# Hybrid decoder step on one core: third expert's weight loads moved behind the first gathers, softmax's maximum and difference moved behind the one-hots

## Chip, cores and metric

The kernel runs on one core of a Trainium2 chip. The metric is the device time of one execution in microseconds. TensorE has two clock levels, 1.2 and 2.4 GHz; the profile gives the granted clock as a share of the higher one.

## What is computed

One layer of a decoder for 536 tokens (16 meta, 512 prompt, 8 sample tokens) of width 1024: a mixer of two branches, then a hierarchical mixture of experts. The change touches only the step from one to the other.

```python
x = x + m                                   # m: mixer output
u = rmsnorm(x, norm2_g)
lg = u @ router_group_w + router_group_b    # 4 groups
le = u @ router_expert_w + router_expert_b  # 4 groups x 4 experts
grp = argmax(lg); p_grp = softmax(lg)[grp]
top_v, top_i = top_k(le[grp], 2); w_top = softmax(top_v)
h = silu(u @ expert_w_gate) * (u @ expert_w_up)      # 16 experts, 1024 x 256
x = x + sum over the token's 2 experts of  p_grp * w_top * (h @ expert_w_down)
y = rmsnorm(x, final_norm_g)
```

## The kernel before

**Two parts.** A first block (the mixer, about 705 us) is written as a list of steps that each engine follows in its own order. Its last steps are the routing. Then comes a loop over rounds (one round here) with the expert passes.

**Routing.** The 536 tokens lie on 128 partitions in 5 tiles. `ranked` (L779) compares the logits of groups and experts with each other and finds each token's experts; for the second part of the tiles (`i` = 1) it ends with softmax's maximum and difference (L811 to L813), on which ACT's exponential waits (semaphore `d_ll`). `placed` (L815) reads each token's place within its expert from PE's sums. `slotted` (L824) makes the one-hot rows (L839) and the pass codes (L835). `slot_products` (L873) on PE multiplies the two, ten small products, and `slots_known` (L842) makes of them the list `ids`: which token stands in which of the 12 passes' 128 slots. Each expert has 96 slots, so a pass of 128 slots holds parts of two experts. All this DVE work stands one behind the other, each operation waiting for the one before.

**Gathers.** The normalised rows u2 were stored to `u_dram` rows (`u_rows` in the profile), x2 to `x_rows`. Once `ids` is known, POOL gathers the rows of passes 0 and 1 (`first_rows`, L886, one indirect DMA of 128 rows x 4 KB each, L883). All later gathers wait in the loop for the buffer of the gather two before (L2065 to L2072).

**Passes on PE.** `to_channels` (L2113) transposes the gathered rows, `gate_up` (L2125) multiplies them by the expert's gate and up weights, `hidden_in` and `down` (L2139, L2147) do the rest. For all but the last three passes ACT scales the result, and POOL adds it to `x_rows` by an indirect DMA (L2076, "the scatter"). When all nine scatters have landed, SP reads `x_rows` back (L2044), POOL gathers the rows that the last three passes still change (L2083), DVE adds and norms them, and the result goes to `out_y` (L2049, L2106).

**Weights.** `load_expert` (L772) asks for two transfers, gate/up (2 MB, L767) and down (1 MB, L770). Six buffers hold six experts. All are asked for on SP's queue, which works through this order:

```python
for i in range(2):
    load_expert(sp, i)            # L982
...
for t in range(2): x2_out(t)      # L997
for t in range(TT): u2_out(t)     # L999
job_done(sp, ("j_out", KD - 1, 1))
load_expert(sp, 2)                # L1002
for t in range(2, TT): x2_out(t)  # L1003
```

In the loop SP waits for both first gathers (L2025), then asks for experts 3, 4 and 5, and from expert 6 on for each as a pass frees its buffer (L2032 to L2038). Where more than one round is needed, a block at the loop's end (L2372) asks for the first three experts of the next.

Of the kernel before, what the change touches and what calls it, by code (L numbers as in the profile page):

```python
# [17 lines left out]
ALU = mybir.AluOpType  # L18
ACT = mybir.ActivationFunctionType
AX = mybir.AxisListType  # L20
# [3 lines left out]
KD = D // P  # L24
# [347 lines left out]
def hybrid_step(nc, I, O):  # L372

    with ExitStack() as ctx:
# [197 lines left out]
        def job_done(eng, step):  # L572
            eng.wait_ge(s_job, JOBS[step] + 1)
# [33 lines left out]
        def bc(a, n):  # L607
            return a.unsqueeze(len(a.shape)).broadcast_to(list(a.shape) + [n])
# [163 lines left out]
        def load_expert(eng, i):  # L772
            load_gu(eng, i)
            load_dn(eng, i)
# [4 lines left out]
        def ranked(dve, v, run, tt, i):  # L779

            t0, t1 = ((0, EARLY), (EARLY, TT))[i]
            rows = slice(t0 * (1 + NG), t1 * (1 + NG))
            if i:
                dve.wait_ge(d_rt, 2)
                run(v.reciprocal(rstd[:, EARLY:TT], rstd[:, EARLY:TT]), d_rc)
            dve.wait_ge(d_lg, i + 1)
            for t in range(t0, t1):
                n = rows_of(t)
                run(v.scalar_tensor_tensor(lg[0:n, t, :], logits(t, n), rstd[0:n, t:t + 1], bias[0:n], ALU.mult, ALU.add))
            x = ll[:, rows]  # L790
            me = bc(x, 4)
            other = x.unsqueeze(2).broadcast_to(list(x.shape[:2]) + [4, 4])
            tt(gt[:, rows], other, me, ALU.is_gt)
            tt(eq[:, rows], other, me, ALU.is_equal)
            tt(eq[:, rows], eq[:, rows], cc("tie", 4, 4).unsqueeze(1).broadcast_to([P, x.shape[1], 4, 4]))
            tt(gt[:, rows], gt[:, rows], eq[:, rows], ALU.add)
            run(v.tensor_reduce(rank.rearrange("p t r e -> p (t r) e")[:, rows], gt[:, rows], AX.X, ALU.add))
            run(v.tensor_scalar(ga[:, t0:t1], rank[:, t0:t1, 0, :], 0.5, None, ALU.is_lt))
            tt(ga[:, t0:t1], ga[:, t0:t1], bc(cc("valid")[:, t0:t1], 4))
            for a in range(2):  # L800
                fv = ff[:, t0:t1, a, :].rearrange("p t (g e) -> p t g e", g=NG)
                run(v.scalar_tensor_tensor(fv, rank[:, t0:t1, 1:1 + NG, :], float(a), bc(ga[:, t0:t1], 4), ALU.is_equal,
                                           ALU.mult))
            tt(selb[:, t0:t1, :], ff[:, t0:t1, 0], ff[:, t0:t1, 1], ALU.add, s=d_sel)

            j = slice(2 * t0, 2 * t1)
            tt(tq[:, t0:t1], ff[:, t0:t1], cc("code").unsqueeze(1).unsqueeze(1).broadcast_to([P, t1 - t0, 2, NE]))
            run(v.tensor_reduce(first[:, j], tq[:, t0:t1].rearrange("p t a e -> p (t a) e"), AX.X, ALU.add))
            run(v.tensor_tensor(first[:, j].rearrange("p (t a) -> p t a", a=2), first[:, j].rearrange("p (t a) -> p t a", a=2),
                                bc(lost[:, t0:t1], 2), ALU.add))  # L810
            if i:  # L811
                run(v.tensor_reduce(mx, ll, AX.X, ALU.max))
                tt(ll, ll, bc(mx, 4), ALU.subtract, s=d_ll)  # L813

        def placed(dve, v, run, tt, i):  # L815

            t0, t1 = ((0, EARLY), (EARLY, TT))[i]
# [83 lines left out]
        def _(sp):  # L901
# [96 lines left out]
                x2_out(t)  # L998
            for t in range(TT):  # L999
                u2_out(t)  # L1000
            job_done(sp, ("j_out", KD - 1, 1))
            load_expert(sp, 2)  # L1002
            for t in range(2, TT):  # L1003
                x2_out(t)

# [614 lines left out]
        def _(dve):  # L1620
# [30 lines left out]
            for step in STEPS:  # L1651
# [258 lines left out]
                elif kind == "j_bc":  # L1910
                    n = step[1]
                    p0, p1, c0, c1 = UNITS[n]
                    job_done(dve, step)
                    for p in range(p0, p1):
                        y = ly[:, p, c0:c1]
                        run(v.scalar_tensor_tensor(y, y, vv("lnw", p), un_ps(kind, n)[:, p - p0, :], ALU.mult, ALU.mult),
                            free if p == p1 - 1 else None)
                elif kind in ("ln_w", "ln_b"):
                    _, n, p = step
                    _, p1, c0, c1 = UNITS[n]  # L1920
                    if n < 6:
                        job_read(dve, ("j_bc", n))
                    for q in [p] if n < 6 else range(p, p1):
                        x, y = tmp[:, q, c0:c1], ly[:, q, c0:c1]
                        if kind == "ln_w":
                            stt(y, y, vv("lnw", q), x, ALU.mult, ALU.mult)
                        else:
                            stt(y, y, vv("lnb", q), bon[:, q, c0:c1], ALU.add, ALU.add)
                elif kind == "ln_g":
                    n = step[1]  # L1930
                    tt(un(ly, n), un(ly, n), un(g_f, n), s=s_ya)
                elif kind == "j_ba":
                    _, m, hf = step
                    job_done(dve, step)
                    if hf == 0:
                        for q in range(2):
                            job_read(dve, ("j_proj", GA0 + m, q))
                            job_read(dve, ("j_bb", m, q))
                    stt(sga[:, m, cols(hf)], sga[:, m, cols(hf)], 1.0, job_ps(step), ALU.add, ALU.mult, s=free)
                    job_read(dve, step)  # L1940
                    tt(merged[:, m, cols(hf)], merged[:, m, cols(hf)], sga[:, m, cols(hf)], ALU.add, s=s_mg)
                elif kind == "j_out":
                    _, m, hf = step
                    dve.wait_ge(s_xr, 16)
                    job_done(dve, step)
                    stt(u[:, m, cols(hf)], job_ps(step), 0.5, u[:, m, cols(hf)], ALU.mult, ALU.add, s=free)
                elif kind == "rt_in":
                    run(v.memset(eps2[:, :], EPS))
                    run(v.tensor_scalar(lost[:, :], cc("valid"), -4096.0, 4096.0, ALU.mult, ALU.add))
                    run(v.memset(ssq, 1.0))  # L1950
                    run(v.memset(lg, 0.0))
                    run(v.memset(cnt, 0.0))
                    run(v.tensor_copy(trib[:, :], cc("tri")))
                    run(v.tensor_copy(oneb[:, :], ones))
                    dve.wait_ge(d_ld, 48)
                    o2 = VEC["norm2_g"]
                    run(v.memset(wr[:, :, 20:32], 0.0))
                    run(v.memset(logt[:, T:TT * P], 0.0))
                    run(v.memset(wsel, 0.0))
                    run(v.memset(wsel[:, 20:21], 1.0))  # L1960
                    tt(quad, ident[:, 0:21], ident[:, 32:53], ALU.add)
                    for i in range(2, 4):
                        tt(quad, quad, ident[:, 32 * i:32 * i + 21], ALU.add)
                    tt(wr[:, :, 0:20], wr[:, :, 0:20], bc(vec[:, o2:o2 + KD], 20), s=d_wr)
                elif kind == "x2":
                    dve.wait_ge(d_rt, 1)
                    run(v.reciprocal(rstd[:, 0:2], rstd[:, 0:2]), d_rc)
                elif kind == "ranked":
                    ranked(dve, v, run, tt, 0)
                elif kind == "slotted":  # L1970
                    placed(dve, v, run, tt, 0)
                    slotted(v, run, 0)
                elif kind == "route":
                    ranked(dve, v, run, tt, 1)
                    placed(dve, v, run, tt, 1)
                    slotted(v, run, 1)
                    slots_known(dve, v, run, at_first)
                    run(v.tensor_reduce(cnt[:, 0:1], bank(6)[:, PS0 + NE * TT:PS0 + NE * TT + NE], AX.X, ALU.max))
                    tt(cnt[:, 1:ROUNDS], cnt[:, 0:1].broadcast_to([P, ROUNDS - 1]), cc("more"), ALU.is_gt)
                    run(v.tensor_reduce(cnt[:, 6:7], cnt[:, 1:ROUNDS], AX.X, ALU.add))  # L1980
                    run(v.tensor_scalar(n_rounds[:, :], cnt[:, 6:7], 1.0, None, ALU.add), d_n)
# [33 lines left out]
        with nc.Fori(0, rounds) as r:  # L2015
# [4 lines left out]
            with nc.Block(no_gpsimd_drain=True) as block:  # L2020
                @block.sync
                def _(sp):
                    sp.wait_ge(d_x, 3)
                    sp.wait_ge(d_lt, 3)
                    for q in range(2):  # L2025
                        at_least(sp, q_g[q], EVERY, 16)
                    load_expert(sp, 3)
                    sp.dma_start(O["retp"], ret_st).then_inc(z_out[1], 16)
                    load_expert(sp, 4)
# [335 lines left out]
            with nc.If(r + 1 < rounds):  # L2365
# [3 lines left out]
                with nc.Block(no_gpsimd_drain=True) as block:  # L2369
                    @block.sync  # L2370
                    def _(sp):
                        for i in range(3):  # L2372
                            load_expert(sp, i)

                    @block.gpsimd
# [85 lines left out]
```

## Time and profile before

| | |
|---|---|
| median of 3 runs | 875.0 us (874.85 to 876.51) |
| the profiled execution: its own time | 876.24 us |
| its span, first to last instruction | 874.7 us |
| mean granted TensorE clock | 0.977 |
| PE busy | 839.2 us (96%) |
| DVE / ACT / POOL busy | 367.6 / 183.7 / 37.6 us |
| DMA moved | 125.29 MB |

Times in the trace count from the span's start. Gather and weight transfers are asynchronous: the row of an issuing instruction shows how long the engine took to ask, and "to landing" is the time from there until the last of the 16 DMA engines has reported. In the chain of waits a DMA row runs from issue to landing. "SPq" is SyncE's queue, "PEld" a weight load into the array. "arena" is the one large on-chip buffer in which most tiles lie.

### The profile page before, as it was taken

How to read it: one execution, taken by the hardware profiler on the slowest of the kernel's cores; microseconds unless marked ns; L12 is line 12 of the kernel's file. 1: busy time of each engine (PE TensorE's matmuls, PEld its weight loads, DVE VectorE, ACT ScalarE, POOL GpSimd, SP SyncE). 2: the span in 40 equal slices, each digit the busy share in tenths (PEclk: the TensorE clock that was granted, in tenths of full speed). 3: DMA queues.
4: the chain of work that ended last, by engine and by line, in shares of the span. 5: the costliest groups of instructions: out<-in, count | busy, mean ns of one | idle time of the engine just before them, and what ended most of it. 6: DMA issues, size and time to landing. Idle time of an engine off the chain costs nothing.

```text
span 874.7 us, 20496 instructions
## 1 busy us (share of the span) xinstructions
PE 839.2 (96%) x9014; PEld 591.5 (68%) x9014; DVE 367.6 (42%) x729; ACT 183.7 (21%) x418; POOL 37.6 (4%) x34
## 2 busy tenths in 40 slices
PE   8999999999999999999999999998999859999994
PEld 6877777787788777777777777776887723333331
DVE  6343333347779554454543343217413441111135
ACT  2111112142322211111111331220004311111134
POOL 0000000000000000000000000000000011122223
PEclk9999999999999999999999999989999959999997
DMA  9432321422211110111013101046362289999965
GB/s 353 153 99 73 107 91 49 170 72 97 73 56 54 37 46 31 39 39 31 35 39 100 50 27 51 3 154 249 146 268 97 73 330 423 384 394 394 391 227 224
DMA packets 30343, 125.29 MB, mean 143 GB/s; under 512 B 5824, under 2 KB 8416, under 8 KB 25392
## 3 DMA queue, kind: packets, MB, share of 16 engines
q1 hardware_dynamic: 25936, 113.03, 34.1%
q0 software_dynamic: 4320, 10.95, 4.3%
q8 instruction: 72, 1.18, 0.5%
q14 instruction: 15, 0.12, 0.0%
HBM read 106.31 MB, written 20.25 MB: 145 GB/s over the span
## 4 chain that ended last, share of the span: by engine, by line
PE 90%; DVE 4%; DMA 3%; issue 2%; ACT 1%; POOL 0%; POOLq 0%; DVEq 0%; ACTq 0%
PE psum L1036 43%; PE psum L1347 9%; PE psum L2135 8%; PE psum L2167 4%; PE psum L1169 2%; PE psum L1208 1%; PE psum L1303 1%; PE psum L1221 1%; PE psum L1125 1%; PE psum L1113 1%; PE psum L2118 1%; PE psum L1218 1%; PE psum L1057 1%; DMA arena<-x_rows,ids 1%; PE psum L1189 1%
## 5 line engine op out<-in xcount | busy, mean ns | idle before, releaser
L1036 PE MATMUL psum<-arena 128*128 128x268 f32 x1600 | 398.8, 397 | 0.2
L1036 PEld LDWEIGHTS psum<-arena 128*128 128x128 f32 x1600 | 294.1, 190 | 75.1 <-issue 12.1
L1638 DVE TENSOR_TENSOR arena<-psum,arena 128x256 f32<-128x256 f32 (+6 forms) x178 | 74.9, 426 | 202.3 <-PE psum L1221 52.3
L1441 ACT ACTIVATE arena<-psum 128x268 f32<-128x268 f32 (+6 forms) x184 | 71.6, 397 | 373.6 <-PE psum L1036 272.9
L1638 DVE TENSOR_TENSOR arena<-arena 128x256 f32<-128x256 f32 (+11 forms) x204 | 102.1, 500 | 42.9 <-ACT arena L1441 31.0
L1347 PE MATMUL psum<-arena 128*128 128x268 f32 x384 | 90.5, 390 | 0.9 <-DVE arena L1641 0.9
L2135 PE MATMUL psum<-arena 128*32 128x512 f32 (+1 forms) x640 | 87.5, 610 | 2.9 <-DVE arena L2288 2.9
L1347 PEld LDWEIGHTS psum<-arena 128*128 128x128 f32 x384 | 71.2, 189 | 16.3 <-DVE arena L1641 1.7
L2288 DVE TENSOR_TENSOR arena<-psum,arena 128x256 f32<-128x256 f32 (+1 forms) x36 | 24.1, 691 | 111.8 <-ACT arena L2202 97.3
L2135 PEld LDWEIGHTS psum<-arena 128*32 128x32 f32 (+1 forms) x640 | 25.5, 117 | 61.3 <-issue 59.7
L1641 DVE SCALAR_TENSOR_TENSOR arena<-arena 128x8 f32<-128x8 f32 (+6 forms) x93 | 49.0, 527 | 12.2 <-DMA arena<-arena 9.1
L883 POOL DMA_INDIRECT arena<-u_rows,ids x12 | 12.5, 1038 | 770.6 <-DVEq L1984 704.2
L1441 ACT ACTIVATE arena<-arena 128x268 f32<-128x268 f32 (+10 forms) x65 | 25.4, 412 | 93.1 <-PE psum L1359 59.1
L2167 PE MATMUL psum<-arena 128*32 128x512 f32 (+1 forms) x288 | 40.2, 596 | 0.0
L1543 ACT ACTIVATE arena<-psum 64x256 f32<-64x256 f32 (+1 forms) x54 | 20.4, 378 | 85.1 <-PE psum L1189 55.0
L1641 DVE SCALAR_TENSOR_TENSOR arena<-arena,psum 128x268 f32<-128x268 f32 (+1 forms) x36 | 18.8, 522 | 27.3 <-PE psum L1036 12.7
L1641 DVE SCALAR_TENSOR_TENSOR arena<-psum,arena 128x268 f32<-128x268 f32 (+2 forms) x23 | 10.4, 451 | 44.6 <-PE psum L1347 39.4
L2167 PEld LDWEIGHTS psum<-arena 128*32 128x32 f32 (+1 forms) x288 | 10.8, 115 | 21.3 <-issue 21.3
L2202 ACT ACTIVATE arena<-psum 128x256 f32<-128x256 f32 x12 | 4.6, 385 | 79.1 <-PE psum L2135 79.1
L2118 PE MATMUL psum<-arena 128*128 128x128 f32 x96 | 13.5, 286 | 7.3 <-DMA arena<-u_rows,ids 7.3
L1208 PEld LDWEIGHTS psum<-arena 32*32 32x32 f32 (+1 forms) x1072 | 11.7, 105 | 12.3 <-issue 12.3
L2217 ACT ACTIVATE arena<-psum,arena 128x1024 f32<-128x1024 f32 x9 | 10.0, 1116 | 37.5 <-PE psum L2167 37.5
(196 smaller groups left out, 677.8 us busy)
## 6 DMA issues: line engine op xcount, KB each, us to landing
arena<-in_w_gu SPq DMA_DIRECT2D x16, 2048.0 KB, 20.8
arena<-in_w_in SPq DMA_DIRECT2D x46, 512.0 KB, 3.5
arena<-in_w_dn SPq DMA_DIRECT2D x16, 1024.0 KB, 19.5
arena<-in_w_out SPq DMA_DIRECT2D x2, 2048.0 KB, 12.3
arena<-in_x SPq DMA_DIRECT2D x8, 268.0 KB, 4.8
arena<-arena SPq DMA_DIRECT2D x16, 134.0 KB, 3.3
arena<-in_x SPq DMA_DIRECT2D x1, 2144.0 KB, 11.1
arena<-in_rets SPq DMA_DIRECT2D x1, 2048.0 KB
```

The lines of the kernel that those rows point to most:

```text
L1036: last = mm(ps, wt[:, i % NW, k, :], rhs[:, k, cols(hf)], start=(k == 0), stop=(k == nk - 1))
L1169: mm(o, bk[full, q, i, p, 0:w], ar[full, q, p, :, 0:w], start=True, stop=True)
L1208: last = mm(psum[g, 2304 + H * p:2304 + H * p + n], ab[c % 2][g, p, 0, rd], tp[c % 2][g, 0, p, 0:n], start=True, stop=True)
L1347: last = mm(ps, w[:, k, :], x[:, k, cols(hf)], start=(k == 0), stop=(k == nk - 1))
L1441: run(nc.scalar.activation(out, in_, fn, **kw), s)
L1543: nc.scalar.activation(tok[c % 2][part, i, :, :], src, ACT.Copy).then_inc(s_toks if s else s_act, 1)
L1638: run(v.tensor_tensor(out, a, b, op), s)
L1641: run(v.scalar_tensor_tensor(out, a, sc_, b, op0, op1), s)
L2118: last = nc.tensor.transpose(psum[:, P * k:P * (k + 1)], ug[:, e % 2, P * k:P * (k + 1)], ident)
L2135: last = mm(bank(2 + i % 2)[part], ue[:, i % 2, k, part], w_gu[x % NWE][:, k, :], start=(k == 0), stop=(k == KD - 1))
L2167: last = mm(bank(down_bank(e) + q)[part], hht(e)[:, f, part], w_dn[x % NWE][:, f, 512 * q:512 * q + 512], start=(f == 0), stop=(f == 1))
L2288: v.tensor_tensor(out, x, y, op).then_inc(s, 1)
```

## The change

`load_expert(sp, 2)` and the wait for the mixer's last product ahead of it leave the first block; the load goes to the loop's SP block, behind the wait for both gathers and ahead of expert 3. The block for a further round loads two experts instead of three. `ranked` loses its last two operations, and the step "route" makes them between `slotted` and `slots_known`.

```diff
@@ -808,10 +808,6 @@
             run(v.tensor_tensor(first[:, j].rearrange("p (t a) -> p t a", a=2), first[:, j].rearrange("p (t a) -> p t a", a=2),
                                 bc(lost[:, t0:t1], 2), ALU.add))
-            if i:
-                run(v.tensor_reduce(mx, ll, AX.X, ALU.max))
-                tt(ll, ll, bc(mx, 4), ALU.subtract, s=d_ll)
-
         def placed(dve, v, run, tt, i):
@@ -998,8 +994,6 @@
             for t in range(TT):
                 u2_out(t)
-            job_done(sp, ("j_out", KD - 1, 1))
-            load_expert(sp, 2)
             for t in range(2, TT):
                 x2_out(t)
@@ -1974,6 +1968,8 @@
                     ranked(dve, v, run, tt, 1)
                     placed(dve, v, run, tt, 1)
                     slotted(v, run, 1)
+                    run(v.tensor_reduce(mx, ll, AX.X, ALU.max))
+                    tt(ll, ll, bc(mx, 4), ALU.subtract, s=d_ll)
                     slots_known(dve, v, run, at_first)
@@ -2024,6 +2020,7 @@
                     for q in range(2):
                         at_least(sp, q_g[q], EVERY, 16)
+                    load_expert(sp, 2)
                     load_expert(sp, 3)
                     sp.dma_start(O["retp"], ret_st).then_inc(z_out[1], 16)
                     load_expert(sp, 4)
@@ -2369,7 +2366,7 @@
                     @block.sync
                     def _(sp):
-                        for i in range(3):
+                        for i in range(2):
                             load_expert(sp, i)
```

SP's queue before, from the end of the mixer into the loop (in_w_gu and in_w_dn are one expert's gate/up and down weights):

```order
82 L995 DMA u_rows<-arena 128x1024 x4
83 L995 DMA u_rows<-arena 24x1024
84 L767 DMA arena<-in_w_gu 128x4096
85 L770 DMA arena<-in_w_dn 128x2048
86 L991 DMA x_rows<-arena 128x1024 x2
87 L991 DMA x_rows<-arena 24x1024
```

The same stretch of SP's queue with the change, on to the first requests in the loop (L2010 to L2014 are the round count, the loop's entry and the wait for the gathers):

```order
83 L991 DMA u_rows<-arena 24x1024
84 L987 DMA x_rows<-arena 128x1024 x2
85 L987 DMA x_rows<-arena 24x1024
86 L1980 UNCONDITIONAL_BRANCH
87 L2010 TENSOR_LOAD n_rounds
88 L2010 ISA x2
89 L2011 UNCONDITIONAL_BRANCH
90 L2017 UNCONDITIONAL_BRANCH
91 L2014 ISA
92 L767 DMA arena<-in_w_gu 128x4096
93 L770 DMA arena<-in_w_dn 128x2048
94 L767 DMA arena<-in_w_gu 128x4096
```

The pair of transfers has gone from between the stores; behind the wait for the gathers expert 2's pair (92, 93) now stands ahead of expert 3's (from 94).

DVE at the end of the routing with the change (L835 makes the one-hots, L841 to L843 are `slots_known`):

```order
541 L835 TENSOR_TENSOR onehot<-arena 128x768
542 L1971 TENSOR_REDUCE arena<-arena 128x25
543 L1632 TENSOR_TENSOR arena<-arena 128x100
544 L841 COPY arena<-psum 128x24
545 L842 SCALAR_TENSOR_TENSOR arena<-arena 128x12
546 L843 TENSOR_SCALAR ids<-arena 128x12
```

The maximum (L1971) and the difference (L1632) stand between the one-hots and the copy that waits for PE's products; before, nothing stood there.

## Rows read from the trace of the kernel before

**Rows 1.** Page, busy us, share of the span, instructions.
```profile
PE 839.2 (96%) x9014; PEld 591.5 (68%) x9014; DVE 367.6 (42%) x729; ACT 183.7 (21%) x418; POOL 37.6 (4%) x34
```

**Rows 2.** Chain of waits, routing to pass 0: start us, us, what.
```profile
698.46 0.27 DVE arena L812
698.75 0.27 DVE arena L1638
...
701.45 0.97 DVE onehot L839
...
702.55 0.43 PE psum L878 x10
...
704.64 8.21 DMA arena<-u_rows,ids
712.90 1.98 PE psum L2118 x8
...
716.38 9.58 PE psum L2135 x64
```

**Rows 3.** Timeline of SP's queue around the gathers: start us, us, instruction.
```profile
697.05 0.54 SPq L767 DMA_DIRECT2D arena<-in_w_gu  x1
...
698.13 1.70 SPq L991 DMA_DIRECT2D x_rows<-arena  x3
...
713.74 0.35 SPq L767 DMA_DIRECT2D arena<-in_w_gu  x1
```

**Rows 4.** Stretches: us, busy of PE, PEld, DVE, ACT, POOL, PEclk, DMA share, GB/s.
```profile
697.00:698.00 1.00, 0.30 (x11) 0.30 (x12) 0.86 (x5) 1.00 (x2) 0.00 (x0) 0.74 1.04 401
712.00:713.00 1.00, 0.10 (x1) 0.10 (x2) 0.00 (x0) 0.00 (x0) 0.00 (x0) 0.50 0.41 160
730.00:735.00 5.00, 5.00 (x26) 1.63 (x24) 0.00 (x0) 0.00 (x0) 0.00 (x0) 1.00 1.04 440
```

**Rows 5.** Single transfers by line: down 11, gate/up 14, gate/up 15, down 15.
```profile
L770 SPq DMA_DIRECT2D arena<-in_w_dn x1: 328/328/328, 787.6 to 787.6; - x1
DMA to landing us min/median/max: 22.8/22.8/22.8
...
L767 SPq DMA_DIRECT2D arena<-in_w_gu x1: 362/362/362, 799.9 to 799.9; - x1
DMA to landing us min/median/max: 26.8/26.8/26.8
...
L767 SPq DMA_DIRECT2D arena<-in_w_gu x1: 328/328/328, 806.5 to 806.5; - x1
DMA to landing us min/median/max: 31.1/31.1/31.1
...
L770 SPq DMA_DIRECT2D arena<-in_w_dn x1: 328/328/328, 823.0 to 823.0; - x1
DMA to landing us min/median/max: 19.5/19.5/19.5
```

**Rows 6.** Timeline and chain, gate/up products of passes 9 and 11, then the end.
```profile
822.94 7.09 PE L2135 MATMUL psum<-arena 128*32 128x512 f32 x64
...
843.21 7.09 PE L2135 MATMUL psum<-arena 128*32 128x512 f32 x64
...
836.95 6.79 DMA x_rows<-arena,ids
843.96 2.51 SPq L2044 DMA_DIRECT2D arena<-x_rows  x5
...
847.41 8.99 DMA arena<-x_rows,ids
```

**Rows 7.** Stretch of one us near the end, columns as in rows 4.
```profile
836.00:837.00 1.00, 1.00 (x6) 0.29 (x5) 1.00 (x1) 0.11 (x1) 0.05 (x1) 1.00 0.25 107
```

**Rows 8.** Page, DMA issues, indirect transfers of 512 KB: count, median us to landing.
```profile
x_rows<-arena,ids POOLq DMA_INDIRECT x12, 11.1
out_y<-arena,ids POOLq DMA_INDIRECT x3, 3.4
```

## The prediction

> **What bounds the kernel now.** I read the page first, then the chain of waits through the routing, the SP queue, DMA by stretches, single transfers with their landings, and last the chain of the end. PE is busy 839.2 us of 874.7 [rows 1], so time comes only from a hole in it, and only if what lies behind the hole can be earlier too. The chain [rows 2] shows the hole: the two DVE operations that the change moves (L812 at 698.46, L1638 at 698.75), the one-hots, PE's products, then 8.21 us in which nothing but the first gather's landing is waited for, then 1.98 us of transposes at 712.90, and at 716.38 the products of pass 0. What the gather waits behind is in [rows 3]: SP asks at 697.05 for the third expert (3 MB: gate/up 2048 KB, down 1024 KB) and at 698.13 for three pieces of x_rows; the fourth expert follows at 713.74, once both first gathers have landed. In [rows 4] the DMA engines are full at 697 (share 1.04) and run empty at 712 (0.41): the gathers land with the last of this backlog.
>
> The other end matters as much. In the pass loop the DMA share is 1.04 at 730 to 735 with 440 GB/s [rows 4]: the weight stream keeps up, but with growing lag. Landings [rows 5]: gate/up 14 asked for at 799.9 took 26.8 us, gate/up 15 at 806.5 took 31.1 (landed 837.6), the last down weights at 823.0 took 19.5 (landed 842.5). By [rows 7] the share at 836 is only 0.25 while those are still under way: about 4 of the 16 engines are late, the others are done. The end hangs on DMA too [rows 6]: the last summed pass's scatter is issued at 836.95 and lands 6.79 later, at 843.74; then come the loads of x_rows and the late gathers (8.99 from 847.41), landed at 856.40; then sums, norms and the last stores to 874.7. PE is not in that chain from 836 on.
>
> **The change, part by part.**
>
> *Maximum and difference.* From the start of one to that of the next are 0.29 us, so the two take 0.58 [rows 2]. In their new place they run while PE makes its ten products. The one-hots end at 702.42 and PE ends at 702.98, 0.56 later, so they fill that time about exactly and cost 0 to 0.1; were PE's cover gone, the cost would be 0.58 again. On ACT the exponential waits for the difference and will run some 1.8 us later. What stands behind it on ACT are copies of products that PE makes only after the slot products, and its own result is first used in pass 0 (L854): nothing. Gain in front of the gathers: 0.55.
>
> *The third expert leaves the stretch ahead of the gathers.* SP's three x_rows requests no longer stand behind two others, come up to 1.0 us earlier (698.13 against 697.05) and are through long before the gathers. The gather, issued at 704.09, then finds idle engines. Bounds for its time: 8.21 (no help at all) and 3.4, the three scatters to out_y at the end, of the same size and queue, with little beside them [rows 8]. I take 4.0, close to that row, because the same thing (an indirect transfer on nearly idle engines) is nearest. It lands at 708.1 instead of 712.85: PE starts **4.8 us** earlier. The granted clock is 0.74 at 697 and 0.50 (1.2 of 2.4 GHz) at 712 [rows 4]; it falls ahead of all that the change moves, so I let transposes and pass 0 keep their durations.
>
> *The third expert enters the stream behind the gathers.* Before, SP's request came 0.9 us behind the first gather's landing, that is at the second's; with empty engines POOL's own issue sets their distance, and I let it be 1.5, so the second lands near 709.6, and SP then asks for expert 2 in place of expert 3: the stream starts 4.1 us earlier (713.74 before) but carries one expert more. Its price: 3.15 MB at the 440 GB/s of 730 to 735 is 7.2 us [rows 4]; from the landing of down 11 (787.6 + 22.8 = 810.4) to that of down 15 (842.5) are four experts in 32.1 us, 8.0 each with their gathers and scatters [rows 5]. I take 7.7, between. Every later landing then moves **3.6 us later** (7.7 - 4.1), while every need moves 4.8 us earlier. Expert 2 itself is first needed in pass 1, which can't start before pass 0's 9.58 us are over (721.2, [rows 2]); its gate/up is asked for at 709.6, and 2 MB at 440 GB/s are 4.8 us: no danger.
>
> *Where that closes.* Pass 9 starts at 822.94 [rows 6] and needs gate/up 13. In order it lands between down 11 (810.4) and gate/up 14 (826.7); of the 5 MB in those 16.3 us it is the first 2, so about 816.9 [rows 5]. New: 820.5 against a need at 818.1. PE waits 2.4 us there, and of 4.8 us 2.4 are left. Pass 11 (843.21) needs gate/up 15: 837.6 + 3.6 = 841.2 against 840.8, another 0.4. So half of PE's gain goes back to waits for weights.
>
> *The last scatter.* It is issued 2.4 earlier, at 834.55, but on the late engines the weights now last until 842.5 + 3.6 = 846.1. Its time lies between 6.79 (now, with weights beside it for 5.5 us on a few engines) and 11.1, the median of all twelve scatters, most of them amid full engines [rows 6, 8]. I take 9.0: no gather stands ahead of it in its queue, as it does with the eleven others, but the late engines are busy all through. It lands at 843.55: -0.2.
>
> *The end.* The last weights' landing moves from 1.5 us ahead of the x_rows loads (843.96) to some 2 us behind their start. That costs between 0 (other engines) and 2.1; data flow only starts a microsecond or more after the issue, so I take 0.4. All behind it moves along.
>
> **Sum.** -0.2 + 0.4 = +0.2 us. The profiled execution (876.24 us, span 874.7) would give 876.4; its own time is 1.2 above the median of the three runs, 875.0, so the forecast there is **875.2**. The reason in a sentence: in front 4.8 us are won, but the DMA engines still have the same bytes to move and stood idle for longer, and the end waits for them.
>
> **Rivals.**
>
> *A, the scatter slips through.* If an engine lets the scatter's few rows in between weights, it takes its 6.79 again from 834.55: landed 841.35, -2.4, and with 0.4 at the end -2.0: **873.0**. For it: now 5.5 of its 6.79 us already lie beside weights. Against it: the 11.1 of the others.
> The Trainium skill, "DMA: Bandwidth & Descriptors", section "Queues, rings and completion order", says that each DMA engine takes turns between its queues, a packet at a time. By that rule this rival is what should happen: the scatter would wait for a packet, not for the backlog, and the time would be near 873. The trace agrees only in part, 6.79 in one place and 11.1 in most.
>
> *B, the stream has slack.* If the stream regains what it lost before pass 9, all 4.8 us reach the end: **870.2**. Against it: share 1.04 in the loop and landings of 26.8 and 31.1 us.
>
> *C, slower: the last scatter and the tail behind a longer stream.* Price of the expert 8.0 and a gather time of 5.0 give 4.9 later for the stream; gate/up 13 comes at 821.8, so PE keeps 1.1; the scatter, issued at 835.85 amid full late engines, takes 10.2 to 11.1 and lands at 846.1 to 846.9: +2.3 to +3.2, say **877.8**. It decides as soon as the scatter takes over 9.2 us from where I put it. For it: the row of 11.1, and engines that fall behind ever further.
>
> *D, the gather is no faster.* If its 8.21 us are its own work, only 0.55 is won and the stream is 7.1 later: gate/up 13 at 824.0, scatter issued near 838.0, the end at **879**. Against it: 3.4 for the same size elsewhere.
>
> **Chances.** A measurement of this kernel tells about 0.2% (1.75 us) from no change. Forecast 0.39, its ends reaching 1.7 us either way; A 0.28, B 0.06, C 0.23, D 0.04. Faster (A, B) 0.34, within 0.2% 0.38, slower (C, D) 0.28, with the edges rounded. The range holds the forecast, A and nearly all of C, and leaves out B and D: 872.4 to 878.0. The likeliest case's own range is 873.5 to 876.7.
>
> **What would show it.** Right: the first gather takes about 4 us, and pass 0 starts near 711.6; the first wait for weights in the whole loop appears ahead of pass 9, 2 to 3 us; last down weights land near 846; last scatter takes 8 to 10 us and lands within 1 us of 843.7; the late gathers land at 856 or 857. Wrong: no wait for weights on PE (B), a last scatter under 7.5 us (A) or over 10 (C), a gather over 7 us (D), or a clock that returns to full earlier than 5 us into pass 0, which the sum leaves out.

## The result, and the profile after

The changed kernel takes **879.8 us** (median of five runs, 877.82 to 880.21) against 875.0 before (874.85 to 876.51): ratio 1.0051, interval 1.0037 to 1.0064. It is slower by 4.8 us, outside the forecast range. The profiled execution took 880.04 us, with a span of 878.5. Three kernels further down (e1, e2, e4) had one execution each in a far slower state, 974 to 2561 us, which their medians leave out.

What lies ahead of the gathers differs by a microsecond or three from one profiled execution to the next, whatever the kernel. So below I often count from the first gather's issue (704.64 before, 703.74 after). From there to the span's end are 170.1 us before and 174.8 after: +4.7, close to the 4.8 of the medians. What the two DVE operations gain lies ahead of that issue and is not in this count.

The chain of waits of the changed kernel (start us, us, what), which answers to [rows 2] and [rows 6]. Lines of after are numbered a few lower: L2115 is the transposes, L2132 the gate/up products.

```profile
703.74 4.35 DMA arena<-u_rows,ids
708.13 1.98 PE psum L2115 x8
...
711.61 8.46 PE psum L2132 x64
...
746.73 36.63 DMA arena<-in_w_gu
783.60 7.09 PE psum L2132 x64
...
819.08 4.82 issue
823.89 8.60 PE psum L2132 x59
...
839.42 8.38 DMA x_rows<-arena,ids
...
851.47 8.70 DMA arena<-x_rows,ids
```

The hole in front has shrunk as meant: the gather takes 4.35 us for 8.21, and PE starts at 708.13 for 712.90. But two waits stand in the pass loop where none stood: before pass 6 (the chain runs back over gate/up 9, asked for at 746.73, landed 783.36) and before pass 9. PE's waits by line say how long (us in total, times, the longest):

```profile
PE psum L2132 <- issue: 4.8, 1, 4.8
PE psum L2115 <- DMA arena<-u_rows,ids: 3.5, 1, 3.5
...
PE psum L2132 <- DMA arena<-in_w_gu: 1.8, 1, 1.8
```

The 4.8 us ahead of pass 9, put down to "issue", are the wait for gate/up 13. The single transfers show it (down 11, gate/up 13, 14, 15, down 15), in the order and the columns of [rows 5]:

```profile
L770 SPq DMA_DIRECT2D arena<-in_w_dn x1: 328/328/328, 781.8 to 781.8; - x1
DMA to landing us min/median/max: 35.2/35.2/35.2
...
L767 SPq DMA_DIRECT2D arena<-in_w_gu x1: 431/431/431, 782.2 to 782.2; - x1
DMA to landing us min/median/max: 41.6/41.6/41.6
...
L767 SPq DMA_DIRECT2D arena<-in_w_gu x1: 361/361/361, 796.0 to 796.0; - x1
DMA to landing us min/median/max: 38.3/38.3/38.3
...
L767 SPq DMA_DIRECT2D arena<-in_w_gu x1: 328/328/328, 802.6 to 802.6; - x1
DMA to landing us min/median/max: 39.1/39.1/39.1
...
L770 SPq DMA_DIRECT2D arena<-in_w_dn x1: 328/328/328, 819.1 to 819.1; - x1
DMA to landing us min/median/max: 28.4/28.4/28.4
```

Gate/up 13 lands at 823.8, and pass 9 starts at 823.89. Against [rows 5], down 11 landed 6.6 us later (817.0 for 810.4), gate/up 14 7.6 later (834.3 for 826.7), 15 by 4.1 and the last down weights by 5.0 (847.5 for 842.5). Stretches, with the columns of [rows 4]:

```profile
702.00:703.00 1.00, 1.00 (x5) 1.00 (x6) 0.77 (x5) 0.22 (x1) 0.00 (x0) 0.50 0.00 0
...
826.00:827.00 1.00, 1.00 (x8) 0.23 (x4) 0.00 (x0) 0.00 (x0) 0.00 (x0) 0.50 0.99 311
```

At 702 the DMA engines move nothing (0 GB/s), which is where the third expert's load used to be. At 826 PE's granted clock is 0.50 in the middle of pass 9: PE had stood still for 4.8 us ahead of it. Pass 9's products took 8.60 us where pass 9 took 7.09 before [rows 6].

**The account**, from the gather's issue. To the last scatter's issue are 132.3 us before and 135.7 after, +3.4: the gather -3.9, pass 0 -1.1 (8.46 for 9.58, since the clock came back to full earlier in it, rows below), the waits ahead of passes 6 and 9 +6.6, the half clock in pass 9 +1.5; that makes +3.1, and 0.3 is left over. Then the scatter took 8.38 for 6.79 (+1.6) and the late gathers 8.70 for 8.99 (-0.3).

The stretches of pass 0 in which the granted clock comes back, first of the changed kernel (pass 0 began at 711.61), then of the kernel before (it began at 716.38):

```profile
714.00:715.00 1.00, 1.00 (x12) 0.36 (x8) 0.89 (x4) 0.00 (x0) 0.00 (x0) 0.82 0.91 377
```

```profile
721.00:722.00 1.00, 1.00 (x12) 0.27 (x8) 0.41 (x1) 0.00 (x0) 0.00 (x0) 0.82 0.95 385
```

Two of these terms belong to this one execution and not to the change. e8 (below) is the changed kernel up to pass 9, and e3 up to the ninth expert's weights; their pass 0 is as long as before, here in the chain of e3, then of e8:

```profile
710.85 9.56 PE psum L2134 x64
```

```profile
711.76 9.93 PE psum L2134 x64
```

In e2, e5, e7 and e8, which keep the whole stream, pass 0 is 1.1 to 1.5 us longer than 8.46, and none has a wait ahead of pass 6. Their only wait for weights is the one ahead of pass 9. It ends when gate/up 13 lands, 119.3 to 119.8 us behind the gather's issue, against 120.1 here. What the shorter pass 0 gained, PE lost again by longer waits, 6.6 us for 4.6 to 5.3 in e2, e7 and e8.

### The profile page after: what moved, and what is told of

Read it like the earlier page. It is cut to its first block, busy times and chain, and to the rows that moved or that the text cites. A ratio compares the mean times of both kernels' runs of the same rounds, so it can differ in the third digit from the quotient of the medians.

```text
span 878.5 us, 20497 instructions
## 1 busy us (share of the span) xinstructions
PE 839.6 (96%) x9014; PEld 593.2 (68%) x9014; DVE 367.6 (42%) x729; ACT 183.7 (21%) x418; POOL 37.6 (4%) x34
## 4 chain that ended last, share of the span: by engine, by line
PE 85%; DMA 7%; DVE 4%; issue 2%; ACT 1%; POOL 0%; POOLq 0%; SPq 0%; DVEq 0%; ACTq 0%
PE psum L1030 43%; PE psum L1341 9%; PE psum L2132 6%; DMA arena<-in_w_gu 4%; PE psum L2164 2%; PE psum L1163 2%; PE psum L1202 1%; PE psum L1297 1%; PE psum L1215 1%; PE psum L1119 1%; PE psum L1107 1%; PE psum L1212 1%; PE psum L1051 1%; PE psum L1183 1%; PE psum L1132 1%
## 5 line engine op out<-in xcount | busy, mean ns | idle before, releaser
L1632 DVE TENSOR_TENSOR arena<-psum,arena 128x256 f32<-128x256 f32 (+6 forms) x178 | 75.0, 426 | 202.6 <-PE psum L1215 52.6
L1632 DVE TENSOR_TENSOR arena<-arena 128x256 f32<-128x256 f32 (+11 forms) x204 | 102.1, 501 | 42.4 <-ACT arena L1435 31.0
L2132 PE MATMUL psum<-arena 128*32 128x512 f32 (+1 forms) x640 | 87.9, 612 | 9.5 <-issue 4.8
L2132 PEld LDWEIGHTS psum<-arena 128*32 128x32 f32 (+1 forms) x640 | 26.6, 118 | 67.5 <-issue 65.9
L1635 DVE SCALAR_TENSOR_TENSOR arena<-arena 128x8 f32<-128x8 f32 (+6 forms) x93 | 49.0, 527 | 12.2 <-DMA arena<-arena 9.0
```

The costliest lines, as they stand in the source:

```text
L1632: run(v.tensor_tensor(out, a, b, op), s)
L1635: run(v.scalar_tensor_tensor(out, a, sc_, b, op0, op1), s)
L2132: last = mm(bank(2 + i % 2)[part], ue[:, i % 2, k, part], w_gu[x % NWE][:, k, :], start=(k == 0), stop=(k == KD - 1))
```

## The experiments

Thirteen kernels ran. For each the profiled execution is counted from the first gather's issue:

| kernel | median us | ratio to before (95%) | first gather | last scatter issued at | it took | to the span's end |
|---|---|---|---|---|---|---|
| before | 875.0 | 1 | 8.21 | 132.3 | 6.79 | 170.1 |
| changed | 879.8 | 1.0051 (1.0037 to 1.0064) | 4.35 | 135.7 | 8.38 | 174.8 |
| e1 softmax only | 874.72 | 0.9995 (0.9986 to 1.0004) | 8.55 | 132.5 | 6.88 | 170.4 |
| e2 load only | 880.06 | 1.0052 (1.0037 to 1.0067) | 4.30 | 136.6 | 6.86 | 174.4 |
| e3 changed, expert 8 left out | 872.71 | 0.9971 (0.9961 to 0.9980) | 4.38 | 128.5 | 8.82 | 168.3 |
| e4 before, expert 8 left out | 873.29 | 0.9980 (0.9967 to 0.9994) | 8.14 | 131.8 | 6.21 | 169.0 |
| e5 kept busy | 878.88 | 1.0042 (1.0029 to 1.0054) | 4.37 | 133.9 | 8.92 | 174.0 |
| e6 down ahead | 874.04 | 0.9993 (0.9983 to 1.0004) | 4.44 | 128.5 | 10.00 | 169.2 |
| e7 first gather | 877.25 | 1.0027 (1.0017 to 1.0038) | 4.32 | 135.1 | 7.90 | 173.6 |
| e8 changed, expert 15 left out | 877.88 | 1.0038 (1.0026 to 1.0050) | 4.32 | 135.3 | 6.08 | 172.5 |
| e9 gate/up ahead | 874.4 | 0.9998 (0.9988 to 1.0007) | 6.24 | 129.8 | 8.77 | 169.4 |
| e10 down 15 last, on e6 | 876.46 | 1.0019 (1.0010 to 1.0029) | 4.23 | 129.6 | 8.08 | 171.6 |
| e11 down 15 last, on before | 876.93 | 1.0024 (1.0013 to 1.0035) | 8.17 | 132.1 | 6.16 | 172.5 |
| e12 changed, plain scatters | 869.8 | 0.9947 (0.9932 to 0.9963) | 4.35 | 128.7 | 5.87 | 165.3 |
| e13 before, plain scatters | 872.92 | 0.9976 (0.9965 to 0.9988) | 8.15 | 132.3 | 3.2 | 168.0 |

The profiled execution is not always a typical one: e6's was 2.2 us and e12's 1.9 us below the kernel's median, e7's 2.7 us above.

**Which half of the change costs.** e1 is the kernel before with the two DVE operations moved alone (they also leave `ranked`):

```diff
                     slotted(v, run, 1)
+                    run(v.tensor_reduce(mx, ll, AX.X, ALU.max))
+                    tt(ll, ll, bc(mx, 4), ALU.subtract, s=d_ll)
                     slots_known(dve, v, run, at_first)
```

> Only the maximum and the difference move; the third expert's request stays ahead of the gathers. Theory W (the weight stream on the DMA engines sets the end, and what the load's move costs is the waits for weights in passes 6 and 9): the gathers are issued 0.5 us earlier but still land with the backlog, so the time is that of before within 0.5 us (874.5 to 875.5), with no wait for weights. Rival S (the softmax move itself costs, through ACT's later exponential or the later row count): 877 or more.

e2 is the changed kernel with these two lines back in `ranked`.

> Only the third expert's request moves; maximum and difference stay where they were. Theory W: all of the loss is here: 879 to 881 (0.5 us later in front than the full change or the same), waits for gate/up weights ahead of passes 6 and 9 of 1 to 2 and 4 to 5 us, last down weights landed near 847. Rival S: 875 to 876.

e1 measured 874.7 (no change), e2 880.1. The loss is all the load's. e2's wait ahead of pass 9 was 5.3 us. The wait ahead of pass 6 that I expected was missing: pass 0 was longer, as said above.

**Does the stream of weights carry it?** In e3 (changed) and e4 (before) the ninth expert's transfers are narrow strips; semaphores and waits stay.

```diff
-            eng.dma_start(we[i % NWE][:, 0:4096], I["w_gu"][expert_at(i)]).then_inc(s_we[i % NWE], 16)
+            n = 64 if i == 8 else 4096
+            eng.dma_start(we[i % NWE][:, 0:n], I["w_gu"][expert_at(i)][:, 0:n]).then_inc(s_we[i % NWE], 16)
```

> The changed kernel, with 64 of 4096 and 64 of 2048 columns of the ninth expert's (number 8) weights loaded, the rest left as the third expert's: 3.1 MB less in the stream, every wait and semaphore as it was. Theory W: the stream is again where it was or ahead of it, no wait for weights in any pass, the clock stays full, last scatter issued 4 to 6 us earlier than before at about 831 to 833, the end at 869 to 872. Rival T (the tail after the last scatter, not the stream, sets the end, whatever the weights do): 876 or more. Rival F (the front's gain is lost on PE elsewhere): above 874 without any wait for weights.

> The kernel before with the same 3.1 MB left out. Theory W: PE never waited for weights there, so only the tail of the stream and the last scatter gain: last down weights landed 5 to 8 us earlier, the scatter 0 to 2 us shorter, the end at 873 to 875. Theory W then has a difference of 3 to 5 us between this and the changed kernel with the same left out, in favour of the changed one; rival T has less than 1.

With one expert less, the changed kernel had no wait for weights, the clock stayed full through the loop, and the last scatter was issued 3.8 us earlier than before (128.5 for 132.3). The time fell by 7.1 us to 872.7, while the same edit of the kernel before gave 1.7. So the stream is what costs. The two also give the price of an expert here directly: counted from the gather's issue, gate/up 13 lands at 109.9 in e3 for 120.1 in the changed kernel, and gate/up 14 at 112.1 in e4 for 122.1 before, so 10.0 to 10.2 us for one expert. But my sizes missed: 872.7 is above the 869 to 872, and the changed kernel's lead over e4 is 0.6 us, within the spread of the runs, not 3 to 5. Under 1 is what rival T forecast for this difference, so the tail does take back the gain in front, though T's 876 or more for e3 is refuted. The rows of the end say where the rest went; the chain of e3, then that of e4:

```profile
831.42 8.82 DMA x_rows<-arena,ids
```

```profile
834.76 6.21 DMA x_rows<-arena,ids
```

e3 issues its scatter 3.3 us earlier, it takes 2.6 longer, and it lands only 0.7 earlier (840.24 for 840.97). What PE won is lost behind DMA engines that still have weights to move. In e4 they had none left: its last down weights landed 13.0 us behind 820.9, at 833.9, and the scatter was issued at 834.76. So 6.2 us is what an adding scatter takes alone; before, its 6.79 held only 0.6 for the weights beside it. Where weights were still moving 6.2 us behind its issue, it landed within 1.3 us of the last of them: 0.3 behind in the changed kernel, 0.2 behind in e3, 0.6 behind in e7 and e10, and 0.9 to 1.3 ahead in e5, e6 and e9.

e8 took out the last expert's weights in the same manner (`if i == 15`), leaving the waits of pass 9 alone.

> The changed kernel, with only narrow strips (64 of 4096 and 64 of 2048 columns) of the last expert's (number 15) weights loaded. Pass 9's wait stays, but behind the last scatter's issue the late engines have less to do. Theory W (the last scatter lands when the late engines are through with the weights): the scatter takes 4.5 to 6 us instead of 8.4, and the end comes 2.5 to 4 us earlier than the changed kernel's, 876 to 877.5. Rival P (only the waits on PE count): 879 or more, since pass 9's wait is the same.

The scatter took 6.08 us instead of 8.38, a little over theory W's 6 and again what it takes alone, with pass 9's wait still 5.1 us. The time fell to 877.9, 1.9 less and just outside my 876 to 877.5; six runs against five leave it open whether the 1.9 is clear of noise, while the scatter's own time is. Both places are real: the waits on PE, and the tail behind the stream.

**The half clock.** e5 fills the wait with five products to an unused bank:

```diff
+                            if x == 13:
+                                for _ in range(5):
+                                    mm(bank(5), ident, w_gu[12 % NWE][:, 0, :], start=True, stop=True)
                             at_least(pe, s_we[x % NWE], loads_of(x % NWE), 16 * (x // NWE + 1))
```

> The changed kernel with five extra products of 128 x 512 on PE, written to an unused bank, between pass 9's wait for expert 12 and its wait for gate/up 13, in the time in which PE only waited (4.8 us). Theory W with the clock: the idle time ahead of pass 9 brought the granted clock to 0.50 for 3.4 us and cost pass 9 1.5 us; kept busy, it stays at 1.00, pass 9's products take 7.1 us instead of 8.6, the last scatter is issued 1.0 to 1.5 us earlier; of that up to 1.5 reaches the end: 878 to 879.5 against 879.8 of the changed kernel. Rival N (the clock falls for another reason, or the tail hides it): 879.5 or more.

Pass 9 in its chain:

```profile
823.64 7.09 PE psum L2135 x64
```

7.09 for 8.60: the clock stayed at 1.00. The median is 0.9 us lower, 878.9, which is not clear of noise (the ratios' intervals overlap); the scatter, issued 1.8 earlier, took 0.5 longer. On PE the clock is 1.5 us of the loss; how much of it reaches the end isn't settled, and it is small.

**How much to move, and when to ask.** e7 asks for the third expert between the two waits for the gathers:

```diff
-                    for q in range(2):
-                        at_least(sp, q_g[q], EVERY, 16)
+                    at_least(sp, q_g[0], EVERY, 16)
                     load_expert(sp, 2)
+                    at_least(sp, q_g[1], EVERY, 16)
```

> The changed kernel, but the third expert is asked for when the first gather has landed instead of both (2.3 us earlier). Theory W: all landings of the stream 1.5 to 2.3 us earlier, the waits ahead of passes 6 and 9 shorter by that, the end at 876.5 to 878.5. If the stream's start did not matter: 879.8 as the changed kernel.

877.25: better by 2.5 us and within my 876.5 to 878.5. But its profiled execution, at 879.93, was the slowest of its twelve. There the stream starts 2.4 us earlier behind the gather's issue, gate/up 13 lands only 0.8 us earlier (I had 1.5 to 2.3), and the wait ahead of pass 9 is 4.6 us. So how the others are faster isn't seen, and the mechanism I gave for it isn't shown.

e6 splits the expert: its down weights go ahead of the gathers, behind all stores, its gate/up weights behind the first gather.

```diff
             for t in range(2, TT):
                 x2_out(t)
+            job_done(sp, ("j_out", KD - 1, 1))
+            load_dn(sp, 2)
...
-                    load_expert(sp, 2)
+                    at_least(sp, q_g[0], EVERY, 16)
+                    load_gu(sp, 2)
+                    at_least(sp, q_g[1], EVERY, 16)
```

> The third expert's two transfers apart: its down weights (1 MB) are asked for ahead of the gathers but behind all stores of rows, where the changed kernel left the DMA engines idle for 4 us; its gate/up weights (2 MB) as soon as the first gather has landed, then, behind the second gather, expert 3. Theory W: the front keeps 4 to 5 us; the stream starts 5.5 us earlier than before with 2 MB more (5.5 us), so its landings stay where they were, no wait for weights or one under 1 us, last scatter issued 3 to 5 us earlier than before and landed with the last down weights; the end at 871.5 to 874. Rival G (any load near the gathers slows them as before): first gather 6 us or more and the time 875 or more.

e9 is its mirror, with gate/up ahead and down behind.

> The mirror of the version with the down weights ahead: gate/up (2 MB) of the third expert behind the stores and ahead of the gathers, down (1 MB) as soon as the first gather has landed. Theory W (gain in front against load moved into the stream): 2 MB take 5 us and run some 2 to 3 us into the gather, which then takes 5.5 to 7 us; the stream gets 1 MB more (2.7 us) and starts 4 us earlier, so its landings are 1 us earlier than before; no wait for weights; the end at 872.5 to 874.5, within 1.5 us of the version with the down weights ahead. If the front's gain were what counts, it would be 1.5 to 2.5 us slower than that version.

The times are 874.04, at the upper edge of the expected 874, and 874.4, inside; neither can be told from before. e6 has all of the gain in front (4.44) and no wait for weights; its scatter is issued 3.8 us earlier and then takes the longest of all:

```profile
829.66 10.00 DMA x_rows<-arena,ids
...
843.33 8.73 DMA arena<-x_rows,ids
```

e9 has half the gain in front, a shorter stream, and ends at the same place. However the 3 MB are split, the last scatter lands 138.5 us behind the first gather's issue (before: 139.1).

**Can the tail be cut by order alone?** e10 (on e6) and e11 (on before) ask for the last down weights behind the loads of x_rows:

```diff
-                        if i > NWE:
+                        if NWE < i < NE:
                             at_least(sp, q_dn, NPASS, last_pass(i - 1 - NWE) + 1)
                             load_dn(sp, i - 1)
...
                         sp.dma_start(xf[0:n, t, :], x2_dram[t * P:t * P + n, :]).then_inc(z_x[t], 16)
+                    at_least(sp, q_dn, NPASS, last_pass(NE - 1 - NWE) + 1)
+                    load_dn(sp, NE - 1)
```

> The version with the third expert's down weights ahead, and besides the last down weights (15, 1 MB), which pass 11 needs only after the late gathers, asked for behind the loads of x_rows instead of in the stream. Theory W (the last scatter lands when the late DMA engines are through with the stream): they are through 2.5 us earlier, the scatter takes 7 to 8 us instead of 10.0, x_rows loads and late gathers start 2 to 3 us earlier; of that 0.5 to 1 goes back, since the last down weights run beside the late gathers; the end at 871 to 873. Rival R (the bytes up to the late gathers' landing set the end, in whatever order): 873.5 to 874.5, no change.

> The kernel before with only the last down weights moved behind the loads of x_rows. There the scatter takes 6.8 us, of which 2 to 2.5 are beside the late engines' last down weights. Theory W: the scatter takes 4.5 to 5.5 us, the end 0.5 to 2 us earlier, 873 to 874.5. Rival R: 875.

Both are slower, by 2.4 and 2.0 us: both of my theories missed. Counted from the gather's issue to the end, both are 2.4 us longer. The scatter is shorter as expected (8.08 for 10.00; 6.16 for 6.79), but the 1 MB now runs beside the late gathers, which are on the path. Their rows, e10's and then e11's:

```profile
844.60 11.89 DMA arena<-x_rows,ids
```

```profile
846.00 12.22 DMA arena<-x_rows,ids
```

11.89 and 12.22 for 8.73 and 8.99: 3.2 us are paid for 0.6 to 1.9 gained. In e10 a wait of 1.5 us ahead of pass 9 came on top, and the scatter was issued 1.1 us later than in e6.

**Why the engines have no slack.** e12 and e13 take the addition out of the nine scatters, so tokens with two experts lose a part of their sum; the packets and bytes of POOL's queue and the order of its transfers stay.

```diff
-                                                yo[:, e % 2, :], None, bounds_check=T - 1, oob_is_err=False,
-                                                compute_op=ALU.add).then_inc(q_yd[e % 2], 16)
+                                                yo[:, e % 2, :], None, bounds_check=T - 1, oob_is_err=False).then_inc(q_yd[e % 2], 16)
```

> The changed kernel with the nine scatters writing their rows instead of adding them to x_rows (the experts' sums are left out where a token has several). If it is the reading for the addition that loads the late engines, gate/up 13 lands 3 us or more earlier than 823.8, the spread between the first and last engine at the last down weights falls from 12 us to under 6, and the end comes at 872 to 876. If the scatters' kind does not matter to the stream, landings and the end stay within 1 us of the changed kernel's (879 to 880.5).

> The kernel before with the nine scatters writing instead of adding (the experts' sums are left out where a token has several). The changed kernel with the same edit took 869.8 us. If the loss of the change is that PE's earlier start has to carry the third expert's load on DMA engines that the additions have already filled, then without additions the change is worth something: here 871.5 to 874, that is 1.5 to 4 us more than 869.8; its own last scatter 5 to 6 us. If the additions only shift both kernels alike, the change costs its 4.8 us here too and this kernel takes 864 to 866.

This is the sharpest test, since the sign turns. Without additions the changed kernel takes 869.8 and the kernel before 872.9: the change is then worth **-3.1 us**, where with them it costs 4.8. The -3.1 rests on four runs against eleven, on two chips, and is less sure than the sign: the intervals of the two ratios (0.9932 to 0.9963, 0.9965 to 0.9988) just fail to overlap. e12 came out below its expected 872 to 876, e13 inside its 871.5 to 874 with a last scatter of 3.2 us for the 5 to 6 I had. Gate/up 13 in e12, then in e13:

```profile
L767 SPq DMA_DIRECT2D arena<-in_w_gu x1: 432/432/432, 780.7 to 780.7; - x1
DMA to landing us min/median/max: 30.9/30.9/30.9
```

```profile
L767 SPq DMA_DIRECT2D arena<-in_w_gu x1: 432/432/432, 788.1 to 788.1; - x1
DMA to landing us min/median/max: 20.4/20.4/20.4
```

From the gather's issue it lands at 110.6 in e12 and 120.1 in the changed kernel; at 103.8 in e13 and 111.8 in e11, which is the kernel before up to there. The additions keep the stream 8 to 9.5 us late by pass 9, in both kernels, and that is the slack the moved load would have needed: e12 has no wait for weights in any pass. The pages of the profiles agree in size. POOL's queue, with the same packets and bytes, takes 4.3% of 16 engines' span in the changed kernel and 3.4% in e12; 0.9% of 870 us is 8 us of all engines. At 836 e13's stretch reads

```profile
836.00:837.00 1.00, 1.00 (x6) 0.35 (x7) 1.00 (x1) 0.17 (x1) 0.00 (x0) 1.00 0.00 0
```

against a share of 0.25 in [rows 7]: e13's last weights landed at 833.4, ahead of the last scatter's issue, so nothing stands beside it, and it takes 3.2 us. Its match with additions is e4's 6.2, alone as well. The late engines have not gone, though. Over the 16 reports of the last down weights the spread from first to last falls from 12.5 us before to 5.7 in e13, and from 12.2 in the changed kernel to 7.5 in e12, where I had forecast under 6. In all four kernels the last four reports stand apart from the other twelve: by 2.9 us before, 2.4 after, 2.0 in e13 and 1.1 in e12.

## Why the prediction was wrong

The mechanism was the right one; a term, the price of an expert in the stream, was too small, and the sign of the sum hung on it.

- **The two DVE operations**: right. Nothing in e1, and in the changed kernel's chain they hide behind PE's products, as worked out:

```profile
700.47 0.97 DVE onehot L835
...
701.58 0.43 PE psum L874 x10
...
702.11 0.19 DVE arena L841
```

  The copy comes 0.10 us behind the end of PE's products (702.01), so they cost 0.1 at most.
- **Gain in front 4.8 us**: right. The gather took 4.35 for the 4.0 taken, PE started at 708.13 for 708.1. Pass 0 was 1.1 us shorter by the clock in the profiled execution, where I let it keep its duration; the runs e2, e5, e7 and e8 have it at 9.5 us or more, so the choice was right for the change and only this execution fell outside it. The stream started at 710.41, 3.3 us earlier, for 4.1.
- **"Every later landing then moves 3.6 us later"**: this is the step that failed. Measured are 6.6 to 7.6 us for the transfers of passes 8 to 10. I had priced an expert at 7.7 us, between the loop's best rate and the last four experts' 8.0. But a transfer's time in this loop holds the gathers and scatters that POOL sends beside it. My reading is that these come with time, not with experts, and thin out beside the last four. The rates fit it: before, down 3 landed at 725.5 and down 11 at 810.4, 10.6 us an expert, against those 8.0; the DMA share from 720 to 820 is 1.02, so the engines are full all the time. A row I had not used, gate/up 3 before, gives the price with all that traffic in it:

```profile
L767 SPq DMA_DIRECT2D arena<-in_w_gu x1: 347/347/347, 713.7 to 713.7; - x1
DMA to landing us min/median/max: 8.5/8.5/8.5
```

  It landed at 722.2, gate/up 15 at 837.6: 12 experts in 115.4 us, 9.6 each. The start's 3.3 and the measured 6.6 to 7.6 make 9.9 to 10.9, and leaving an expert out (e3, e4) gave 10.0 to 10.2. With 9.6 and a start 3.3 earlier the same sum gives +6.3: gate/up 13 at 823.2 instead of 820.5, and a kernel that is slower.
- **Waits for weights**: the place was right for pass 9 (2.4 forecast, 4.8 measured; 4.6 to 5.3 in e2, e7 and e8), pass 11 had none of the 0.4, and pass 6, which I did not work out, had 1.8, in this execution alone.
- **The clock**: I named its return in pass 0 as left out, but not that a wait of some length in the loop would bring it down: 1.5 us in pass 9. With the 3.4 us by which pass 9 started later than forecast (823.89 for 820.5), that is the 4.9 by which the last scatter's issue missed.
- **The last scatter 9.0 us**: 8.38, right in kind and nearly in size. Its issue was forecast at 834.55 and came at 839.42. I took its 6.79 as a time with weights beside it for 5.5 us; e4's 6.2 shows that nearly all of it is the scatter's own. Rival A, the scatter slipping through, is refuted where it counts: e3 8.82, e6 10.00. The Trainium skill ("DMA: Bandwidth & Descriptors", section "Queues, rings and completion order") has each engine take turns between its queues by packets. Turns or none, the last scatter took 1.6 to 3.2 us more where more weights stood beside it; the traces don't show the turns themselves.
- **The end, +0.4**: the late gathers took 0.3 less. Nothing lost there.
- **Rival C** was nearest in its mechanism (a dearer expert, a later scatter), at 877.8, and still 2 us short: it took 8.0 for the expert. I gave it 0.23; the row of 9.6 would have made it the forecast. Rival D's 879 is nearer as a number, but its cause, a gather that stays at 8.21 us, did not happen (4.35).

What stays open: why about four of the sixteen engines fall behind the others. e12 and e13 show that the additions bring about half of the spread between the first and the last engine, and not why it is these engines. The same page of the Trainium skill, section "Latency and other measured facts", says that two of the sixteen usually run slower and gives only a guess at the reason; the share of 0.25 here speaks of about four.

## What to carry to other kernels

When a load is moved out of the way of a critical transfer, price it where it goes: by the long-run rate of that stretch with all the traffic that keeps coming there, and compare that with the slack of each later need, late in the stream above all. A DMA share near 1 over 100 us (here 1.02) warns that a gap made elsewhere has to be paid back later. The tail is set by the last engines to finish, so other work on them, here additions done by the DMA engines, can decide whether an edit far away gains or loses. And a term read from one profiled execution, such as pass 0's 1.1 us here, is worth looking up in the other runs before it is put down to the change.

## What was not expected

- A scatter that adds costs the DMA engines far more than one that writes: nine of them, 0.5 MB each, held the weight stream back by 8 to 9.5 us, and one with no weights beside it took 6.2 us adding (e4) and 3.2 us writing (e13).
- One MB beside the late gathers cost them 3.2 us (8.99 to 12.22), more than its 2.4 us at the loop's 440 GB/s; moving it there from the stream saved at most 1.9.
- A pause of 4.8 us on PE brought the granted clock to 0.50 into the next products and cost 1.5 us on top; a pause of 1.8 us ahead of pass 6 did not (its products took 7.09). Pauses of 4.6 to 5.3 us in e7, e8 and e2 cost 1.4 to 2.8 us in the same way (8.46 to 9.92 for 7.09).
